# Operand tiles at multiples of 512 bytes, an early Exponential table in the odd mixer, and query turns ahead of the root in the even mixer

## The reference, cut to what matters

```python
# first block: a gated recurrence beside sparse attention, then a gated feed-forward
h = rms_norm(x, g); proj = h @ w_in
y_a = (rg_lru(conv(xr)) * gelu(gr)) @ w_rnn_out
y_b = sparse_attention(q, k, v, iq, ik, iw) @ w_att_out
x = x + rms_norm((sigmoid(g_a) * y_a + sigmoid(g_b) * y_b) @ w_o, g)
x = x + rms_norm((silu(h @ w_gate) * (h @ w_up)) @ w_down, g)      # width 2816
# second block, for l in (0, 1)
x = x + 0.5 * swiglu(rmsnorm(x), ffn1[l])                          # width 2816
if l == 0:                                                         # the even mixer
    u, v = split(gelu(a_uv)); out_a = u * (w_s @ rmsnorm(v) + b_s)
    q, k = rope(rmsnorm(q)), rope(rmsnorm(k))                      # 4 heads of two maps, 64 wide
    w = softmax(q0 @ k0.T / 8) - lam * softmax(q1 @ k1.T / 8)
    out_b = rmsnorm(w @ v)
else:                                                              # the odd mixer
    out_c = softmax(q @ k.T) @ v_c    # 8 heads, q and k of width 96 out of low-rank projections
    out_d = softmax(qd @ kd.T) @ vd   # 8 heads of width 64 on 2 key heads
x = x + concat(out_1, out_2) @ w_out
x = x + 0.5 * swiglu(rmsnorm(x), ffn2[l])
```

## Time and profile before

| | us |
|---|---|
| median of 3 runs | 1451.47 |
| the 3 runs | 1451.47, 1453.86, 1451.29 |
| profiled execution, time | 1453.35 |
| profiled execution, span | 1451.5 |
| mean granted clock | 0.988 |
| PE busy | 1405.4 |
| DVE busy | 886.9 |
| ACT busy | 753.8 |

### The profile page before, as it was taken

The page is one execution under the profiler, slowest core; times in us unless marked ns, Lnnn a source line. Parts: engine busy times, 40 slices in busy tenths (PEclk is TensorE's granted clock), DMA queues, the critical chain, the costliest instruction groups (busy, mean ns, idle before and its releaser), DMA issues.

```text
span 1451.5 us, 18277 instructions
## 1 busy us (share of the span) xinstructions
PE 1405.4 (97%) x6978; PEld 1178.5 (81%) x6978; DVE 886.9 (61%) x1485; ACT 753.8 (52%) x1179; POOL 14.2 (1%) x21
## 2 busy tenths in 40 slices
PE   6999999899999899999979999999999979999999
PEld 6799777788888788888858888888888868888887
DVE  5888866665555745556876555555455575655543
ACT  4567754464444544445755544444444477644442
POOL 1000000000000000000000000000000000000000
PEclk9999999999999999999989999999999989999999
DMA  8556434465564565554625555655555540465561
GB/s 271 151 154 178 155 102 146 151 210 184 166 206 142 173 204 186 187 183 157 201 59 174 189 177 189 201 175 188 188 175 179 158 153 1 131 217 188 169 209 58
DMA packets 131767, 242.56 MB, mean 167 GB/s; under 512 B 8544, under 2 KB 21472, under 8 KB 131680
## 3 DMA queue, kind: packets, MB, share of 16 engines
q1 hardware_dynamic: 130768, 239.15, 51.1%
q0 software_dynamic: 624, 2.10, 0.5%
q10 hardware_dynamic: 288, 0.14, 0.0%
HBM read 240.31 MB, written 1.05 MB: 166 GB/s over the span
## 4 chain that ended last, share of the span: by engine, by line
PE 92%; DVE 4%; ACT 2%; issue 0%; DMA 0%; SPq 0%; DVEq 0%
PE PB L467 84%; PE PB L500 3%; PE PB L717 2%; PE PB L640 1%; PE PB L701 1%; DVE WL L403 1%; PE PB L645 0%; DMA X<-in_x_dram 0%; PE PB L1150 0%; DVE AT0l L868 0%; ACT WH L413 0%; DVE SM L545 0%; DVE SM L544 0%; DVE SM L543 0%; ACT SR L675 0%
## 5 line engine op out<-in xcount | busy, mean ns | idle before, releaser
L403 DVE TENSOR_TENSOR WL<-RAW,WH 128x1024 fp32r<-128x1024 f32 (+1 forms) x453 | 537.0, 1214 | 224.5 <-ACT WH L413 224.3
L413 ACT ACTIVATE WH<-RAW 128x1024 fp32r<-128x1024 f32 (+1 forms) x453 | 466.9, 1055 | 299.9 <-PE PB L467 299.1
L467 PE MATMUL PB<-WH,AT0h 128*128 128x512 f32 (+3 forms) x1328 | 507.0, 382 | 6.6 <-DVE WL L403 3.7
L467 PE MATMUL PB<-WL,AT0h 128*128 128x512 f32 (+3 forms) x1328 | 499.1, 376 | 0.0
L467 PE MATMUL PB<-WH,AT0l 128*128 128x512 f32 (+3 forms) x1328 | 498.8, 376 | 0.0
L467 PEld LDWEIGHTS PB<-WH,AT0h 128*128 128x128 f32 x1328 | 252.7, 190 | 52.2 <-DVE WL L403 4.2
L467 PEld LDWEIGHTS PB<-WH,AT0l 128*128 128x128 f32 x1328 | 252.4, 190 | 44.8
L467 PEld LDWEIGHTS PB<-WL,AT0h 128*128 128x128 f32 x1328 | 252.7, 190 | 43.0 <-issue 0.7
L467 PE MATMUL PB<-WH,FTh 128*128 128x512 f32 x440 | 174.1, 396 | 0.0
L467 PE MATMUL PB<-WH,FTl 128*128 128x512 f32 x440 | 172.5, 392 | 0.0
L467 PE MATMUL PB<-WL,FTh 128*128 128x512 f32 x440 | 170.8, 388 | 0.0
(11 more groups left out here) (320 smaller groups left out, 1113.0 us busy)
## 6 DMA issues: line engine op xcount, KB each, us to landing
RAW<-in_ffn_w_gu_dram SPq DMA_DIRECT2D x88, 512.0 KB, 4.6
RAW<-in_ffn_w_gu_2b_dram SPq DMA_DIRECT2D x88, 512.0 KB, 4.6
RAW<-in_w_in_dram SPq DMA_DIRECT2D x48, 512.0 KB, 4.4
RAW<-in_ffn_w_down_dram SPq DMA_DIRECT2D x44, 512.0 KB, 4.2
RAW<-in_ffn_w_down_2b_dram SPq DMA_DIRECT2D x44, 512.0 KB, 4.2
RAW<-in_w_ffn_gate_dram SPq DMA_DIRECT2D x22, 512.0 KB, 4.4
RAW<-in_w_ffn_up_dram SPq DMA_DIRECT2D x22, 512.0 KB, 4.8
RAW<-in_w_ffn_down_dram SPq DMA_DIRECT2D x22, 512.0 KB, 4.3
```

The costliest lines, as they stand in the source:

```text
L403: e.tensor_tensor(o, s, h, ALU.subtract), th, loaded[i], hl_free[i % NHL])
L413: th = op("act", lambda e, o=WH[i % NHL][:, 0:m], s=RAW[i % NRAW][:, 0:m]: e.activation(o, s, ACT.Copy), loaded[i], hl_free[i % NHL])
L467: e.matmul(o, l, r, start=s, stop=p, skip_group_check=feature_major)
```

## The change

There are four edits. The **layout**: the constant tiles RW, RP, CO and SM are declared first, SM with 938 elements where it had 896 (the rest is padding), and XR goes to the end of the first block's tiles. In the compiled kernel after, X, AT0, AT1, AT3, RAW, WH, WL, SR, ID, FT and nearly all other tiles of the first block and the even mixer start at multiples of 512 bytes; the odd mixer's G, Q, K, V, KT, PT leave 256. The **even mixer**: `diff` begins its query turns when the queries are rotated, and waits with the score products and L671 until the root is there. The **odd mixer**: one Exponential of one column of the identity stands at its start, with the result unused. The **planner**: `onward` adds 0.1 us where no generator is due.

```diff
+        RW = sb("RW", [128, ROWS["n"]])
+        RP = sb("RP", [128, 2, NROPE])
+        CO = sb("CO", [128, COLS["n"]])
+        SM = sb("SM", [128, 938])
         X = sb("X", [128, 2, D])
         AT0h = sb("AT0h", [128, 8, S], F32R)
         AT0l = sb("AT0l", [128, 8, S], F32R)
...
         SR = sb("SR", [128, 4, 512])
-        CO = sb("CO", [128, COLS["n"]])
-        RW = sb("RW", [128, ROWS["n"]])
-        RP = sb("RP", [128, 2, NROPE])
         ID = sb("ID", [128, 128])
         JK = sb("JK", [128, 2, 512], mybir.dt.bfloat16)
-        SM = sb("SM", [128, 896])
...
             B1["GB"] = sb("GB", [128, 2, D], F32, c1)
-            B1["XR"] = sb("XR", [128, 8 * 259], F32, c1)
             B1["GR"] = sb("GR", [128, 8, S], F32, c1)
...
             B1["T2"] = sb("T1b", [128, 160], F32, c1)
+            B1["XR"] = sb("XR", [128, 8 * 259], F32, c1)
...
             def onward():
                 pump()
-                Q.at["pe"] = min([due[g] for g in side if due[g] > Q.at["pe"]], default=Q.at["pe"])
+                Q.at["pe"] = min([due[g] for g in side if due[g] > Q.at["pe"]], default=Q.at["pe"] + 0.1)
...
                     give(b, tq)
                     yield tq
+                    while roots and not roots():
+                        yield Q.at["pe"] + 0.2
+                    if roots:
+                        yield roots()
                     yield from room()
...
                             k = dve(lambda e: e.scalar_tensor_tensor(nm, mx, -1.0, qs(blk, hs), ALU.mult, ALU.mult), k,
-                                    kwaits)
+                                    roots() if roots else kwaits)
...
                     k6 = dve(lambda e: e.tensor_tensor(x2, x2, t1, ALU.add), k4, k5)
+                    flags[i] = k6
                     yield from calm(4.0)
                     y, k = roots(i, 8, 64)
...
-                    turned_[i] = [k, k6]
+                    turned_[i] = k
 
                 def diff():
-                    while 0 not in turned_ or 1 not in turned_:
+                    while 0 not in flags or 1 not in turned_:
                         yield
                     yield turned_[1]
                     kk = stacked_keys(KT, lambda b, i: QK[:, b, 512 + i * 128:640 + i * 128],
                                       [(i, i) for i in range(4)], turned_[1], kz2)
-                    yield turned_[0]
+                    yield flags[0]
...
-                        [kk, turned_[0], klam, bar], None, lam=lamc, many=(6, 4.0), late=kv2,
+                        [kk, flags[0], klam, bar], None, lam=lamc, many=(6, 4.0), late=kv2,
+                        roots=lambda: turned_.get(0),
...
                 rt_ = lambda: [stage["rt"], bar]
+                early = small(1)
+                op("act", lambda e: e.activation(early, ID[:, 0:1], ACT.Exp), ("d_id", 16))
                 OUT, CQ, G, QM, KM, V3 = (B3[x] for x in ("OUT", "CQ", "G", "Q", "K", "V"))
```

More of the change, by code:

```diff
@@ L605, in stacked_keys, with attention @@
                 return toks
-            def attention(units, d, dv, scale, PT, QT, slots, q, kt, v, kwaits, owaits, bias=None, lam=None, many=None, chosen=None, qs=None, sums=None, late=None, rings=None, first=0):
+            def attention(units, d, dv, scale, PT, QT, slots, q, kt, v, kwaits, owaits, bias=None, lam=None, many=None, chosen=None, qs=None, sums=None, late=None, rings=None, first=0, roots=None):
                 ns, npt, nq = len(slots), PT.shape[1], QT.shape[1]
```

## The result

The kernel after takes 1455.49 us (median of 10 runs, 1452.94 to 1459.05), the kernel before 1452.41 (10 runs, 1451.29 to 1454.44): a ratio of 1.0020 with a 95% interval of 1.0011 to 1.0029. It is slower by 3 us (1.6 to 4.2). Forecast was 1449.8, a gain of 1.7; the time lies in the stated range of 1412 to 1458, but the sign is wrong. The profiled execution after took 1459.05 us, span 1457.2. It is the slowest of the ten, so its length is not the median's; what each place in it takes can be read.

A forecast was written before the change was run, and what follows sets the result against it. PE bounds the kernel, busy 1405.4 of 1451.5 us. Layout -2.9, even mixer -2.9 and odd mixer +4.1 sum to -1.7, added to the median 1451.47: 1449.8 us, range of 8 in 10 from 1412 to 1458.

The forecast's parts named there:

- The even mixer's **-2.9: Even mixer: first output turn's wait gone and less time at half clock, together -2.9 us, between -4.1 and +1.
- The odd mixer's **+4.1: Odd mixer: +1.9 up to L631's wait, +1.2 at the end, +1.0 for the clock; between -1.3 and +6.
- its term for the tail, **+1.2: End of odd mixer: twelve products no longer cover ACT's copies and DVE's scaling, +1.2 us, bounds 0 and +2.8.
- FT falling to AT0's 227 ns: 512-column products on FT: starts fall from 229 to 227 ns once all share one phase, -2.9 us.
- The rivals with the fixed part gone: Matmuls: the 13 ns fixed part goes, 1390 us, chance 0.15; or a part of it goes, 1419, 0.13.
- the second rival: Matmuls: fixed part falls from 13 to the 7 ns AT3 shows at 256 columns, 34 us, 1419; chance 0.13.
- The step that took its wait of 2.33 as -2.3: Even mixer, first output turn (L1438): inputs ready long before its new place, so its 2.33 us wait goes, -2.3.
- The -0.6 for the clock: Even mixer, between the two output turns: work at half speed could run in half the time, -0.6, bounds 0 and -1.2.
- -1.3 at the first L701: Odd mixer, first L701: the 1.28 us table load moves from before the first Exponential into ACT's idle time, -1.3.
- Forecast +1.9: Odd mixer up to L631 and the L705 behind: PE waits there, swallowing the early load, +1.9, between -1.3 and +2.2.
- The +1.0 for a low stretch: Odd mixer: more idle time could hold the clock low for one further stretch, +1.0 us, bounds 0 and +1.7.
- "the odd mixer's order costs its upper bound": Odd mixer: PE idles at L631 and in the uncovered tail, +6.0; with layout worth nothing 1454.6 us; chance 0.12.

The follow-up runs named there:

- e11_ft128: Kernel before with 320 bytes of padding ahead of FT, so FT leaves 128 of 512 as AT0 does: 1451.28 against 1451.71 us, ratio 0.9990.
- e3_even: Kernel before with the even mixer's edit alone: 1452.65 against 1453.93 us, ratio 0.9992.
- e9_layout_even: Kernel before with the layout and the even mixer's edit, without the early Exponential and the planner's 0.1 us: 1449.07 against 1451.71 us, ratio 0.9985.
- e8_fill_table: Early Exponential in the order of before, with 18 and 28 unused transposes in front of the odd mixer's two L701: 1453.64 against before's 1453.92 us, ratio 0.9997.
- e2_table_order: Kernel before with the early Exponential known to the planner and the planner's 0.1 us, no layout or even mixer edit: 1459.59 against 1453.93 us, ratio 1.0042.
- e7_fill_after: Kernel after with 18 and 28 unused transposes in front of the odd mixer's first two L701: 1456.52 against before's 1453.92 us, ratio 1.0018.
- e6_fill_before: Kernel before with 24 and 28 unused transposes in front of the odd mixer's first two L701: 1454.01 against 1453.92 us, ratio 1.0005.
- e4_table_only: Kernel before with the early Exponential recorded behind the planner's back, instruction order otherwise kept: 1455.84 against 1453.93 us, ratio 1.0015.
- e10_layout_even_fill: e9_layout_even with unused transposes, 32 before the even mixer's last output turn and 13 before each of two L855: 1447.62 against before's 1451.71 us, ratio 0.9966.
- e1_layout: Kernel before with the layout alone, in the instruction order of before: 1450.73 against 1453.93 us, ratio 0.9982.

## Why the prediction was right or wrong

The mechanisms of the prediction were mostly there; sizes were wrong, and they turned a forecast of -1.7 into about +3. Two terms did it. The even mixer's **-2.9** took the wait of 2.33 us as gained and measured -1.2, because two new waits of 1.90 and 0.47 took its place. The odd mixer's **+4.1** measured +6.1, most of all because its term for the tail, **+1.2**, came out at some 3.3.

**Layout: right.** Forecast -2.9 us by FT falling to AT0's 227 ns; measured 227 ns and -2.6 us (-4.2 to -1.2), of which the feed-forwards show 2.1 in the profile. The rivals with the fixed part gone (1390 and 1419) had 0.28 of the chance between them and are refuted: products at multiples of 512 still start 227 ns apart, and 120 for 256 columns. The few narrow ones on AT3, from whose 114 ns the second rival took its 7 ns, start 120 apart in after (five in 0.60 us from 1185.26). The reason I gave, one phase shared by all operands, is neither shown nor refuted: in the kernels with 227 ns (after, e11_ft128) all share one, in those with 229 and 233 FT stands apart from WH, and no run had all at a third address. The figure of 215.7 ns in the Trainium skill's page "TensorE: Matmul & The Clock Gate", section "Wait — 56ns, not 53.3ns?", was reached by no operand address of these runs. The Trainium skill's page "SBUF — State Buffer", section "Who interferes with whom", names only the shared port as a place of contention; from that I derived a price of 0 for an address, and the runs show 2 to 6 ns for each matmul.

**Even mixer: half right.** Forecast -2.9 with bounds of -4.1 and +1, measured -1.2 (-2.5 to +0.1). The step that took its wait of 2.33 as -2.3 failed: the wait did go, but I took the other gaps to shift about at 0, with +1.5 as the bound. The transposes L705 now wait 1.90 us for DVE's subtraction of the two maps (L689), and a product with V 0.47. That the moved work had been cover for these steps is how I read the order; no run undid it by itself. The -0.6 for the clock is not borne out either: the clock of this window was 0.83 in after as in before, 0.89 in e3_even and 0.85 in e9_layout_even.

**Odd mixer, the load: wrong.** Forecast -1.3 at the first L701. Its wait fell from 3.20 to 2.39, 0.8 us, and I said the gain would be swallowed by the wait behind. But I had no price for what it could do on the way: alone, it costs 2.2 us. TensorE stands still once more in front of L575, and the granted clock stays at 1.2 GHz for some 14 us in place of 7; that the one brings the other is argued, that the low clock is the cost is shown by e8_fill_table, where the load is worth 0.

**Odd mixer, the order: right in kind, too small.** Forecast +1.9, +1.2 and +1.0, together +4.1 with the load's -1.3 in it; measured +6.1 (e2_table_order), and +7.8 without the load. By e7_fill_after, whose clock is nearly full, the order's waits alone make 5.8. In its profile I summed, behind 1213 us, by how much the starts lie further apart than the same kind of matmul usually does: some 3.3 us in the tail, with no such gap in before (in after it is 3.2). So the term for the tail was mis-sized: 1.2, a guess under half of a cover that I had put at 2.8, measured 3.3, above its bound. The middle is what remains, 2.5, for my 1.9. There the forecast was close: the third group of probabilities starts 58.6 us behind weight matmul 4800 in e7_fill_after where before has 58.8, with two score products and three query turns still to do. The +1.0 for a low stretch is the 1.0 between the profiles of after and e7_fill_after; their ratios (1.0020 and 1.0018) don't tell them apart. But I had named DVE's chain as what L631 waits for, and it was not: L1697's counterpart ended at 1203.85 in after, and L631 waited to 1206.29 for ACT's copies of the keys, since L575, moved behind L721 and L644, ended late. The Exponentials of the third group had their scalars at 1205.03 and started at 1206.13, behind the same copies. So the middle's size was near for a wrong reason, which is luck: I looked at DVE's chain and not at what the move did to L575 and its copies, for which L631 waits too. The split of the middle from the tail rests on the profile; neither was undone alone.

**The rival** "the odd mixer's order costs its upper bound", 1454.6 with a chance of 0.12, is near what happened, by a slightly different path: +6.1 for the mixer where it had +6.0. It had a layout worth nothing with it, which is wrong, and an even mixer of -2.9, which was -1.2. The parts now sum to -2.6 - 1.2 + 6.1 = +2.3, and the whole measured +3 (1.6 to 4.2).

**The clock: its price depends on the place.** In the kernel before, 7 us at half clock in the odd mixer cost nothing, as e6_fill_before shows; in e4_table_only 14 us cost 2.6. In the even mixer the full clock is worth some 3.7 us of the profile, and by the ratios the three fillers together 2.8.

## What to carry to other kernels

Price a stretch at low clock by who is late behind it: where another engine's chain sets the next step it can cost nothing, and where products stand ready it costs up to half of itself. Filling the idle time in front can then be a cheap gain; of the three places filled here for that, two paid and one did not. When a planner's cost is edited, even by one instruction that is hidden, read the new order for what stood as cover at the end and has moved, and follow the copies of each group that has moved, not only the inputs of the one that waits. Let both operands of such a matmul leave the same remainder of 512 bytes, as the two good cases here (0 and 128) have it, and don't expect more from the boundary itself.

## What the runs showed of the hardware

The distance between fast fp32 matmuls depends on where the stationary operand starts, for 512 columns: 227 ns with both operands at 0 or both at 128 of 512 bytes, 229 with it at 320 and the weights at 128, 233 with it at 32 and the weights at 0. No address tried brought it under 227.

TensorE's clock fell not only behind idle time. In before it was granted 0.74 on average from 27 to 40 us, with PE busy without a gap from 15 us on, and the fall came amid a run of 48 matmuls of only 72 columns (25.9 to 33.2 us). The same instructions in the profile of e11_ft128 had 1.00, and the first block took 287.20 us there against 290.96. Windows of the two, before and then e11_ft128:

```profile
27.00:40.00 13.00, 13.00 (x64) 11.73 (x64) 6.15 (x27) 3.75 (x4) 0.00 (x0) 0.74 0.42 141
```

```profile
27.00:40.00 13.00, 13.00 (x78) 11.47 (x78) 8.26 (x32) 4.70 (x5) 0.00 (x0) 1.00 0.40 131
```

Some tiles lie at other addresses in e11_ft128, but that is not the reason: e9_layout_even and e10_layout_even_fill have the same layout and the same instructions up to the first filler at 277 us, and their windows are

```profile
27.00:40.00 13.00, 13.00 (x56) 11.53 (x56) 6.33 (x28) 3.48 (x4) 0.00 (x0) 0.61 0.34 120
```

```profile
27.00:40.00 13.00, 13.00 (x77) 11.39 (x77) 8.62 (x33) 4.34 (x5) 0.00 (x0) 1.00 0.31 105
```

By matmul 1100 the second is 4.9 us ahead (256.50 against 261.38 us). So one and the same order may or may not meet a low stretch, and executions of one kernel differ with the clock that they were granted: of the 29 runs of before beside e1_layout, the seven with a mean clock of 0.991 took 1449.6 to 1451.7 us and the 22 with 0.987 to 0.989 took 1452.9 to 1454.6. The length of one profiled execution can't carry a verdict of 2 us. The odd mixer's stretch can, since it scatters by less than half a us with the order of before, but for e4_table_only.
